# Expert weights in six slots of 2 MB instead of twelve of 1 MB, in a two-layer diffusion block on one Trainium2 core

## The reference, cut to what matters

```python
def ec_moe(h, router_w, w1, w3, w2):
    B, T, D = h.shape
    cap = EC_CAPACITY * T // N_EXPERTS
    aff = jax.nn.softmax((h @ router_w).astype(jnp.float32), axis=-1)
    gate, idx = lax.top_k(jnp.swapaxes(aff, 1, 2), cap)
    xs = jax.vmap(lambda hb, ib: hb[ib])(h, idx)
    hid = jax.nn.silu(jnp.einsum('becd,edf->becf', xs, w1)) * jnp.einsum('becd,edf->becf', xs, w3)
    y = jnp.einsum('becf,efd->becd', hid, w2) * gate[..., None].astype(h.dtype)
    return jax.vmap(lambda ib, yb: jnp.zeros((T, D), h.dtype).at[ib.reshape(-1)].add(yb.reshape(-1, D)))(idx, y)
```

## Time and profile before

| | |
|---|---|
| median of 3 runs | 2096.3 us (2091.82 to 2097.45) |
| profiled execution, its own time | 2090.86 us |
| its span, first to last instruction | 2089.1 us |
| granted TensorE clock, mean | 0.938 |
| PE busy | 1816.9 us (87%) |
| PE weight loads busy | 1076.4 us (52%) |
| DVE, ACT, POOL busy | 697.4, 435.3, 115.5 us |
| moved by DMA | 565.53 MB, mean 271 GB/s |

### The profile page before, as it was taken

How to read it: one execution, slowest core, us unless ns; L and a number is a source line. 1 busy time by engine, 2 the same in 40 slices (tenths; PEclk the granted TensorE clock), 3 DMA queues, 4 the chain that set the end, 5 groups by cost and what they waited for, 6 DMA issues and landing times.

```text
span 2089.1 us, 24721 instructions
## 1 busy us (share of the span) xinstructions
PE 1816.9 (87%) x9928; PEld 1076.4 (52%) x9928; DVE 697.4 (33%) x1117; ACT 435.3 (21%) x760; POOL 115.5 (6%) x157
## 2 busy tenths in 40 slices
PE   5999999999999899999999799999997666656654
PEld 3878756666787433333333488877885121111111
DVE  3362354643334422222211454556455010101001
ACT  3222333332222200000000432444333000000000
POOL 2070000000000000000000241000000000000000
PEclk9999999999999999999999999999998877778788
DMA  9433233344446799999999843444788899999997
GB/s 321 128 90 92 86 107 125 96 133 131 143 140 272 303 405 421 422 422 422 422 422 422 232 141 98 130 131 131 226 267 359 349 421 421 421 422 422 421 421 288
DMA packets 233132, 565.53 MB, mean 271 GB/s; under 512 B 12152, under 2 KB 159760, under 8 KB 183888
## 3 DMA queue, kind: packets, MB, share of 16 engines
q1 hardware_dynamic: 230736, 557.73, 69.9%
q0 software_dynamic: 1760, 4.40, 1.2%
q10 hardware_dynamic: 544, 2.10, 0.2%
HBM read 563.11 MB, written 1.07 MB: 270 GB/s over the span
## 4 chain that ended last, share of the span: by engine, by line
PE 70%; DMA 22%; DVE 4%; issue 2%; SPq 1%; ACT 1%; POOL 0%; POOLq 0%; ACTq 0%; DVEq 0%
PE PS L764 44%; PE PS L1201 17%; DMA nab<-in_moe_w 13%; DMA e_wr<-in_moe_w 7%; PE PS L1152 2%; PE PS L814 2%; DMA ring<-in_w_mod 2%; PE PS L939 1%; PE PS L961 1%; SPq L741 1%; PE PS L1179 0%; PE PS L1085 0%; PE PS L1162 0%; DMA ring<-in_w_in 0%; DVE arena L1763 0%
## 5 line engine op out<-in xcount | busy, mean ns | idle before, releaser
L764 PE MATMUL PS<-hTr,wr 128*128 128x512 f32 (+1 forms) x2688 | 517.4, 349 | 6.6 <-DVE hTr L1691 4.0
L764 PEld LDWEIGHTS PS<-hTr,wr 128*128 128x128 f32 x2688 | 429.8, 191 | 75.1 <-issue 7.2
L1201 PE MATMUL PS<-arena 128*32 128x512 f32 (+1 forms) x960 | 303.6, 700 | 83.6 <-DMA nab<-in_moe_w 40.3
L1639 DVE TENSOR_TENSOR wr<-ring,wr 128x1024 fp32r<-128x1024 f32 x152 | 187.9, 1237 | 226.2 <-ACT wr L1269 226.0
L1269 ACT ACTIVATE wr<-ring 128x1024 fp32r<-128x1024 f32 x152 | 160.9, 1058 | 297.9 <-PE PS L764 279.0
L1201 PE MATMUL PS<-e_h,arena 128*64 128x512 f32 (+1 forms) x624 | 165.8, 701 | 48.7 <-DMA arena<-in_moe_w 42.9
L1201 PE MATMUL PS<-arena,e_h 128*64 128x512 f32 (+1 forms) x576 | 171.3, 705 | 34.0 <-DMA nab<-in_moe_w 16.9
L764 PE MATMUL PS<-wr,hTr 128*128 128x512 f32 x816 | 187.9, 390 | 4.7 <-DVE hTr L1893 2.6
L1201 PEld LDWEIGHTS PS<-arena 128*32 128x32 f32 (+1 forms) x960 | 82.6, 139 | 210.0 <-issue 205.2
L764 PEld LDWEIGHTS PS<-wr,hTr 128*128 128x128 f32 x816 | 151.9, 188 | 38.1 <-DVE wr L1639 3.4
L2063 DVE TENSOR_TENSOR x<-x,PS 128x512 f32<-128x512 f32 x80 | 55.0, 688 | 237.1 <-PE PS L764 237.1
(11 more groups left out here) (186 smaller groups left out, 1819.8 us busy)
## 6 DMA issues: line engine op xcount, KB each, us to landing
arena<-in_moe_w SPq DMA_DIRECT2D x192, 1024.0 KB, 18.1
e_h<-in_moe_w SPq DMA_DIRECT2D x90, 1024.0 KB, 18.6
ring<-in_w_in SPq DMA_DIRECT2D x136, 512.0 KB, 4.1
e_wr<-in_moe_w SPq DMA_DIRECT2D x64, 1024.0 KB, 20.5
ring<-in_w_mod SPq DMA_DIRECT2D x94, 512.0 KB, 5.2
nab<-in_moe_w SPq DMA_DIRECT2D x32, 1024.0 KB, 21.8
ring<-in_w_br SPq DMA_DIRECT2D x64, 256.0 KB, 4.9
ring<-in_w_out SPq DMA_DIRECT2D x16, 512.0 KB, 4.2
```

The source lines that it names most:

```text
L764: return nc.tensor.matmul(o, a, b, start=first, stop=last)
L1201: ins = nc.tensor.matmul(PS[g * R:(g + 1) * R, bank + h, :], src[:, k, g * R:(g + 1) * R], space[:, kk * D + h * 512:kk * D + (h + 1) * 51 ...
L1639: nc.vector.tensor_tensor(wr[:, j % 2, 1, :], ring[:, slot, :], wr[:, j % 2, 0, :].bitcast(f32), ALU.subtract).then_inc(w_lo.sem, 1)
```

## The change

- **Pieces.** A piece is now 512 rows of a matrix: 2 MB, partition p holds rows 4p to 4p+3 (16 KB together). A matrix has two pieces. There are six slots of 2 MB in the same 12 MB. `expert` has two steps j with four rows kk each, and waits for the pieces of all G experts of the pack at the start of a step.
- **One-time slots.** Two in layer 0: ring places 0 to 3, and ring places 4 and 5 with `par`. A third in layer 1: the context rows of x with half of `work`, all unused there. So 8 pieces (16 MB) in layer 0 and 9 (18 MB) in layer 1 are in place before the first expert matmul. `par` of layer 1 is loaded once the one-time slots are used.
- **Order of release.** Three slots (6 MB) before the output projection, three after it. The last G pieces of a layer are loaded in halves.
- **Columns by stream.** In layer 0 the 128 columns are ordered by stream, then expert. A product's matmul of 64 columns becomes two of 32. `combT` has two tiles; a combine is eight matmuls of 64 rows each, in pairs on the two halves of the array, and is done in two parts, before and in the middle of the second product. Its banks are more, so in layer 1 it no longer waits for DVE's adds.
- **First step.** The first product starts its first step when half of `xsT` is written.
- **Order of the rows.** As the layout of rows is by fours, the modulation matmuls of parts 3 and 4 read their weights by a stride, and the transposes (`paired`) take every fourth column.
- Layer 1's first norm takes the tiles in the order 0, 2, 1, 3, as the combine now finishes them. The `memset` of `selg` is gone.

```diff
 NSLOT = 6
-ESLOT = 12
-EXTRA = NSLOT // 2
+ESLOT = 6
+EARLY_SLOTS = 3
+EXTRA = (2, 3)
...
-    return v.rearrange("t (j p r) -> t j r p", p=128, r=2)[:, k // 2, k % 2, :]
+    return v.rearrange("t (j p r) -> t j r p", p=128, r=4)[:, k // 4, k % 4, :]
...
-        ring = sb("ring", [128, NSLOT, 1024])
-        x = sb("x", [128, 4, D])
+        ring_par = sb("ring_par", [128, 8192])
+        ring = ring_par[:, 0:NSLOT * 1024].rearrange("p (a b) -> p a b", a=NSLOT)
+        par = ring_par[:, NSLOT * 1024:NSLOT * 1024 + P_ALL]
+        x_work = sb("x_work", [128, 4 * D + 9 * 512])
+        x = x_work[:, 0:4 * D].rearrange("p (a b) -> p a b", a=4)
+        work = x_work[:, 4 * D:].rearrange("p (a b) -> p a b", a=9)
...
-        espace = [arena[:, 0, :], arena[:, 1, :], arena[:, 2, :], arena[:, 3, :], nab_all[:, 0:2048],
-                  arena[:, 4, :], arena[:, 5, :], e_wr[:, 0, :], e_wr[:, 1, :], e_h[:, 0, :], e_h[:, 1, :], e_h[:, 2, :]]
-        xspace = [ring[:, 2 * e:2 * e + 2, :].rearrange("p a b -> p (a b)") for e in range(EXTRA)]
+        espace = [unit_of(0, 2), unit_of(2, 2), unit_of(4, 2), e_wr[:, :, :].rearrange("p a b -> p (a b)"),
+                  e_h[:, 0:2, :].rearrange("p a b -> p (a b)"), e_h[:, 2:4, :].rearrange("p a b -> p (a b)")]
+        xspace = [ring_par[:, 0:4096], ring_par[:, 4096:8192], x_work[:, 2 * D:2 * D + 4096]]
         xsT = unit_of(6)[:, 0:1024].rearrange("p (a b) -> p a b", a=KD)
         hid = unit_of(6)[:, 1024:2048]
         sil = unit_of(7)[:, 1024:2048]
         toks = sil
-        hidT = e_h[:, 3, 0:1024].rearrange("p (a b) -> p a b", a=KD)
-        ysb = e_h[:, 3, 1024:2048]
-        combT = nab_all[:, 2048:2560].rearrange("p (a b) -> p a b", a=4)
-        selg = nab_all[:, 2560:3072].rearrange("p (a b) -> p a b", a=4)
+        hidT = nab_all[:, 0:1024].rearrange("p (a b) -> p a b", a=KD)
+        ysb = nab_all[:, 1024:2048]
+        late_w = nab_all[:, 0:2048].rearrange("p (a b) -> p a b", a=2)
+        combT = nab_all[:, 2048:2304].rearrange("p (a b) -> p a b", a=2)
+        selg = nab_all[:, 2560:2816].rearrange("p (a b) -> p a b", a=2)
         afT = unit_of(6)[0:32, 0:256]
...
-                def load_pack(i, first):
-                    n = 0
-                    for w in experts:
-                        for j in range(4):
-                            for g in range(G):
-                                src = w[l, ds(i * (G * 4) + (g * 4 + j), 1), :, :].rearrange("k p n -> p (k n)")
-                                extra, s, turn = e_place(n, first)
-                                if first and late < end:
-                                    if n == 7:
-                                        load_items(late, end)
-                                        load_late(l)
-                                    if n == ESLOT + EXTRA:
-                                        store_gates(l, MS[l] - 1)
-                                        spread_gates(l, MS[l] - 1)
-                                if extra is not None:
-                                    if extra == 0:
-                                        for m in range(end - NSLOT, end):
-                                            sync.wait_ge(*items[m][3])
-                                    sync.dma_start(xspace[extra], src)\
-                                        .then_inc(extra_loaded[extra], 16)
-                                else:
-
-                                    sync.wait_ge(e_freed[s], i * G + (l * (e_uses[s] + 1) + 1 + turn))
-                                    sync.dma_start(espace[s], src)\
-                                        .then_inc(e_loaded[s], 16)
-                                n += 1
-
-                load_pack(0, True)
-                with sync.Fori(1, NP[l]) as i:
-                    load_pack(i, False)
-                sync.wait_ge(extra_used, EXTRA * (l + 1))
-
-            sync.wait_ge(e_freed[1], L * (e_uses[1] + 1))
+                def rows_of(i, n):
+
+                    return experts[n // (2 * G)][l, ds(i * (G * 2) + (n % G * 2 + n // G % 2), 1), :, :]\
+                        .rearrange("k p n -> p (k n)")
+
+                def load_slot(i, n, first):
+
+                    _, s, turn = e_place(l, n, first)
+                    sync.wait_ge(e_freed[s], i * G + (freed_before(l, s) + 1 + turn))
+                    sync.dma_start(espace[s], rows_of(i, n)).then_inc(e_loaded[s], 16)
+
+                def load_extra(n):
+
+                    e = n - ESLOT
+                    if e == 0:
+                        for m in range(end - NSLOT, end):
+                            sync.wait_ge(*items[m][3])
+                    elif e == 1:
+                        sync.wait_ge(*shift_logits.at(l, 1))
+                    else:
+                        sync.wait_ge(*pv.at(l, NB[l]))
+                        sync.wait_ge(*m_lo.at(l, KD))
+                    sync.dma_start(xspace[e], rows_of(0, n)).then_inc(extra_loaded[e], 16)
+
+                def load_last():
+
+                    for g0 in range(0, G, 2):
+                        for hh in range(2):
+                            for g in (g0, g0 + 1):
+                                n = 5 * G + g
+                                _, s, turn = e_place(l, n, False)
+                                if hh == 0:
+                                    sync.wait_ge(e_freed[s], (NP[l] - 1) * G + (freed_before(l, s) + 1 + turn))
+                                cols_ = slice(hh * 2048, (hh + 1) * 2048)
+                                sync.dma_start(espace[s][:, cols_], rows_of(NP[l] - 1, n)[:, cols_])\
+                                    .then_inc(last_loaded[hh], 16)
+
+                for n in range(EARLY_SLOTS):
+                    load_slot(0, n, True)
+                if late < end:
+                    load_items(late, end)
+                    load_late(l)
+                else:
+                    load_extra(ESLOT + 2)
+                    load_extra(ESLOT)
+                for n in range(EARLY_SLOTS, ESLOT):
+                    load_slot(0, n, True)
+                if late < end:
+                    load_extra(ESLOT)
+                load_extra(ESLOT + 1)
+                if late < end:
+                    store_gates(l, MS[l] - 1)
+                    spread_gates(l, MS[l] - 1)
+                for n in range(ESLOT + EXTRA[l], 6 * G):
+                    load_slot(0, n, True)
+                with sync.Fori(1, NP[l] - 1) as i:
+                    for n in range(6 * G):
+                        load_slot(i, n, False)
+                for n in range(5 * G):
+                    load_slot(NP[l] - 1, n, False)
+                load_last()
+                sync.wait_ge(extra_used, sum(EXTRA[:l + 1]))
+
+            sync.wait_ge(e_freed[3], freed_before(L, 3))
...
+                by_fours = w.rearrange("q (a p b c) -> q a b p c", a=2, b=2, c=2)
                 for j in range(PQ):
-                    i = nc.tensor.matmul(o[32 * j:32 * j + 32, :], cond[:, k, :], w[:, j * MQ:(j + 1) * MQ],
+                    if mod_of(l, n)[1] in (3, 4):
+                        dst = o[32 * j:32 * j + 32, :].rearrange("q (p c) -> q p c", c=2)
+                        src = by_fours[:, j // 2, j % 2, :, :]
+                    else:
+                        dst, src = o[32 * j:32 * j + 32, :], w[:, j * MQ:(j + 1) * MQ]
+                    i = nc.tensor.matmul(dst, cond[:, k, :], src,
                                          start=(k == 0), stop=(k == KD - 1),
                                          tile_position=(0, 32 * j), skip_group_check=True)
                 i.then_inc(mod_step.sem, 1)
@@ -819,12 +891,12 @@
...
-                for s in range(7):
+                for s in range(EARLY_SLOTS):
...
-                def expert(i, first, w):
+                def expert(i, first, last, w, between=None):
 
                     bank, done_ = ((0, h1_sum), (2, h3_sum), (4, y_sum))[w]
                     src = xsT if w < 2 else hidT
-                    n = 4 * G * w
-                    for j in range(4):
+                    n = 2 * G * w
+                    for j in range(2):
+                        if j == 1 and between is not None:
+                            between()
+                        halves = last and w == 2 and j == 1
                         for g in range(G):
-                            extra, s, turn_ = e_place(n + g, first)
+                            extra, s, turn_ = e_place(l, n + g, first)
                             if extra is not None:
-                                pe.wait_ge(extra_loaded[extra], 16 * (l + 1))
-                            else:
-                                pe.wait_ge(e_loaded[s], i * (16 * G) + 16 * (l * e_uses[s] + turn_ + 1))
-                        for kk in range(2):
-                            k = 2 * j + kk
+                                pe.wait_ge(extra_loaded[extra], 16 * (1 if extra >= EXTRA[0] else l + 1))
+                            elif not halves:
```

(107 more changed lines are left out.)

96 lines of the change are left out of this document (51 added, 45 removed).

## The result

| | before | after |
|---|---|---|
| median (5 runs each, side by side) | 2092.48 us (2091.77 to 2097.45) | 2124.95 us (2119.31 to 2127.24) |
| span of the profiled execution | 2089.1 us | 2123.9 us |
| granted TensorE clock, mean | 0.938 | 0.921 |
| PE busy | 1816.9 us | 1766.5 us |
| moved by DMA | 565.53 MB | 565.58 MB |

The account below looks back on a forecast made before the run. The prediction took layer 0's experts as bound by DMA with PE close behind, layer 1's by DMA alone. Its terms, -1.6 - 1.7 - 0.9 + 23.1 - 1.7 = +17.2 on 2090.9, plus 5.4 to the median, gave 2113.5 us, range 2098 to 2127.

Parts of the forecast that it names:

- The rate of a 16 KB packet: DMA transfers: 621 ns a packet against 630 for two of 8 KB, so 422 GB/s becomes 428.
- Layer 0: Layer 0's experts: no such loop, DMA at 426 GB/s or more, PE's last group ending at 1167.1; -1.6 us.
- between the layers: Combine to layer 1's norm: DVE's eight adds set the pace instead of the combine's matmuls; -1.7 us.
- the tail: End of the kernel: the last group's halves leave 3.7 us of PE after the landing instead of 5.43; -1.7 us.
- the hidden rows: Layer 0's last pack: 4.5 us of PE between the second product's last group and the third product.
- Layer 1's mixer: Layer 1 before its experts: the first product starts at half of xsT; -0.9 us.
- the loop of layer 1: Layer 1's experts: with six slots, refills wait for PE's group, so a group takes 21.4 us; +23.1 us.
- PE's group: Loop term in layer 1: 64 matmuls, mostly starting at a low clock, take 9.15 us (8.35 to 9.95).
- The rest of the period: Loop terms in layer 1: issue 0.15, around the transfer 2.2, two transfers 9.8, landing to PE 0.13 us.
- The loop doesn't close: Rival, layer 1: PE's group at full clock, below 7.3 us, lets DMA rule; 2080 us; chance 0.20.
- The loop just closes: Rival, layer 1: PE's group at its lower bound, 8.35 us, 20.6 a group; 2097, no change; chance 0.17.
- The modulation's strides: Rival, modulation: strided reads of weights cost time; 2133 us with the loop; chance 0.03.

Follow-up runs that it names:

- e4: The changed kernel with four unused matmuls at the start of every group of layer 1, after its wait: 2202.94 us, ratio to before 1.0512.
- e2: The changed kernel with eight recycled 2 MB slots in layer 1, two one-time slots being refilled there: 2076.35 us, ratio to before 0.9908.
- e8: e2 with each 2 MB piece loaded by two transfers of 1 MB with 8 KB packets: 2088.57 us, ratio to before 0.9977.
- e1: The changed kernel with twelve slots of 1 MB and 8 KB packets, the last pieces no longer loaded in halves: 2083.87 us, ratio to before 0.9948.
- e3: The changed kernel, six slots, with unused matmuls before layer 1's groups while PE would wait: 2106.95 us, ratio to before 1.0059.
- e7: e2 with 16 MB instead of 18 loaded ahead of layer 1's experts: 2081.31 us, ratio to before 0.9942.
- e10: A repeat of e2, eight recycled 2 MB slots in layer 1 of the changed kernel: 2078.58 us, ratio to before 0.9918.
- e9: e2 with unused matmuls in layer 1 while PE would wait for a group: 2077.75 us, ratio to before 0.9922.

## Why the prediction was right in sign and half the size

**The mechanism: right, and shown.** The predicted loop is there (refills in fours, a gap in each period), it costs time through PE (e4), and it goes with two more slots and nothing else changed in kind (e2). The size was not right: +17.2 us was forecast, and the spans differ by 34.8.

**The rate of a 16 KB packet: right.** From 800 to 1130 us the trace has 9706 packets, 1080 of them small, over 16 engines at a share of 1.006: 330 × 16 × 1.006 / 8626 = 616 ns each, against 621 predicted; 428 GB/s as predicted. e8 prices it, together with the size of the transfers: 10 to 12 us of the whole time.

**Layer 0, between the layers, the tail: right.** PE's last product in layer 0 ends at 1153.02 + 14.00 = 1167.0 (predicted 1167.1). That it agrees to 0.1 us is luck: the landing came 0.9 us later than predicted (1142.3 against 1141.4) and the hidden rows took 3.5 us instead of 4.5, and in the profiles of e1, e2, e3, e7 and e10, alike in layer 0 but for e1's slots, the same product ends between 1163.7 and 1170.3. From there to layer 1's projections at 1188.64 it is 21.6 us against 23.1 before, −1.4 (predicted −1.7). After the last group's start 15.6 us are left against 17.5, −1.9 (predicted −1.7). The trace of the combine between the layers:

```profile
1167.88 1.99 PE L830 MATMUL PS<-nab 64*128 64x512 f32 x8 [0.92 <-DVE nab L2180]
...
1170.44 2.23 PE L830 MATMUL PS<-nab 64*128 64x512 f32 x8 [0.57 <-DVE x_work L2153]
```

Eight matmuls of 64 rows, sixteen records, take 4.2 us in two parts, against 7.70 before and 3.7 predicted.

**Layer 1's mixer: −0.9 predicted, +1.8 measured** (432.9 us from the projections to the first expert product, against 431.1). In the profiles of e1, e2, e3, e7, e9 and e10, whose mixers are the same, this stretch took from 429.5 to 436.7 us, so +1.8 is scatter as far as the runs tell, and −0.9 could not be seen.

**The step that was mis-sized: the loop of layer 1.** Predicted, 9.15 + 0.15 + 2.2 + 9.8 + 0.13 = 21.4 us, and +23.1 in all. Measured, 22.1 us, and from the first expert product to the last landing's group 486.8 us against 448.7: **+38.1**. Term by term:

- PE's group: 9.25 us in the mean (8.4 to 10.0), predicted 9.15. Good to 0.1.
- The rest of the period: 22.12 − 9.25 = 12.9 us, predicted 12.3. Here is the miss. The first 2 MB transfer after the hole, at 1895.81, took 7.8 us to its landing, of which 4.90 are its time at 428: 2.9 us around it, not 2.2. I took the 2.2 from a transfer of 1 MB in the same place. The second transfer landed 12.7 us after the first was issued, 9.8 + 2.9.
- 0.7 us a period, twenty times, is 14.6 us, and 0.5 more until the fourth group (44.3 us from the first start against 43.8). That is the 15.0 between +23.1 and +38.1.

The sum by these terms: −1.7 − 1.4 + 1.8 + 38.1 − 1.9 = +34.9, the difference of the spans (2123.9 − 2089.1 = 34.8). Against the forecast's +17.2 that is 17.7 too much. The median had been set 7.2 us above the span by the three runs of before; with more runs the changed kernel's lies 1.1 above its own, which takes 6.1 back. 17.7 − 6.1 = 11.6, and the 12 us are accounted for.

**The rivals.** *The loop doesn't close* gave 2080 and rested on PE's group at the full clock. e3 is that case built: the groups took 7.05 us, and the kernel came to 2107, not 2080. So this rival had its deciding point (a group below 7.3 us) in the wrong place, by 0.7 us at least: with 2.9 around a transfer, the loop would first close at 6.6, under the 7.0 that a group of 64 matmuls takes at the full clock, and e3's period of 20.9 puts it lower still. Its 0.20 was too much. *The loop just closes* fell with it. *The modulation's strides* cost nothing that e1 and e2 show, and the trace says the same: from 60 to 700 us, where layer 0's parts 3 and 4 are two of six, a record of the modulation takes 390 ns in the mean before and 393 after. The part was not run by itself.

The Trainium skill (TensorE: Matmul & The Clock Gate, HAM oscillation) holds that a PE which waits for DMA at each tile loses its clock. The change shows it, 0.73 in the window. Keeping PE busy gave back 18 us with six slots (e3) and nothing with eight (e9): the low clock made the loop dearer, and the loop stayed without it.

**Left open.** Why 2.9 us lie around the first 2 MB transfer and 2.2 around one of 1 MB. Why e3's period is 20.9 us and not 20.2, its two slow groups counted. Columns by stream and strides were not undone one by one.

**The best version** is the change with eight recycled slots in layer 1 (e2, e10): 0.8% under the kernel before and 2.3% under the change. Its parts, by e7 and e8: 10 to 12 us from the larger packets and transfers, 3 to 5 from the 2 MB more ahead of layer 1.

## What to carry to other kernels

Count slots in the units in which they are freed: those still free when a group has landed must hold DMA's work for as long as the next group takes on the engine, plus the time around one transfer, or engine and DMA work in turn. Here two free slots covered 9.8 us where 9.3 + 0.2 + 2.9 were wanted, and four covered it at any clock. Take it as a lower bound: in e3 the same count left 0.3 us uncovered, and 1.3 a period were lost. A few matmuls added to each group tell in one run whether the engine is on the path: 78 us with six slots, 0 to 7 with eight.

## What the chip did that I had not expected

- The time around the first transfer after a hole was not the same for both sizes: 4.7 − 2.5 = 2.2 us for 1 MB, 7.8 − 4.9 = 2.9 us for 2 MB. The Trainium skill (DMA: Bandwidth & Descriptors, Anatomy of one DMA) has it as a constant of about 2.0 us, for transfers issued by GpSimd. These, issued by SP, differ from that, and by the constant the loop would have been forecast 0.9 us a period too short.
- After the hole the rate did not return at once: 377, 87, 319 and 377 GB/s in four slices of 0.565 us, then over 400. With 1 MB transfers it was 149 and 223 in two slices of 0.55 us, then 432 and 447 (before, from 1627.5 us). And it fell in e3, where the refills came before DMA ran dry.
- A TensorE clock of 0.75 instead of 0.98 cost nothing while the stream set the pace (2078.58 against 2077.75 us), and about 1.3 us a group where it did not.
